# Hybrid pooling and retention step on one core: keys and values turned by VectorE in 32 by 32 blocks instead of by TensorE

## The reference

```python
proj = jnp.einsum('bld,de->ble', rmsnorm(x, g_norm), w_in)      # 1024 -> 10240 columns
u_p, z_p, q, k, v, z_r, gates = jnp.split(proj, IN_SPLITS, axis=-1)
qh, kh = rope(q), rope(k) * RET_QK_DIM ** -0.5                  # 4 heads of 256
o, s_new = retention(qh, kh, vh, s0)                            # values: 4 heads of 512
# one chunk: scores = q @ k.T * decay;  o = scores @ v + (q * decay) @ s
#            s_new  = decay * s + k_dec.T @ v
y_ret = (groupnorm(o) * gn_ret * silu(z_r)) @ w_branch_ret
x_out = x + (sigmoid(gate_p) * y_pool + sigmoid(gate_r) * y_ret) @ w_out
```

## Time and profile before

| | |
|---|---|
| median of three runs | 2835.89 us (2834.78 to 2838.54) |
| profiled execution | 2833.37 us, its span 2831.6 us |
| projection / rest of the span | up to about 1690 us / from there |
| TensorE busy | 2782.2 us, 98% |
| VectorE, ScalarE, GpSimd busy | 64%, 40%, 24% |
| DMA, mean over the span | 195 GB/s |

### The profile page before, as it was taken

One profiled execution on the slowest core, in us unless ns is written; L12 is line 12 of the kernel. 1 busy time (PEld: TensorE's weight loads), 2 busy tenths in 40 slices (PEclk: granted clock), 3 DMA queues, 4 the chain that ended last, 5 costly groups with the idle time before them and its releaser, 6 DMA issues.

```text
span 2831.6 us, 36714 instructions
## 1 busy us (share of the span) xinstructions
PE 2782.2 (98%) x13504; PEld 2249.1 (79%) x13504; DVE 1808.3 (64%) x2588; ACT 1126.4 (40%) x1901; POOL 684.8 (24%) x456
## 2 busy tenths in 40 slices
PE   6999999999999999999999999999999999999998
PEld 5888888888877777777777787877887888788876
DVE  8667566667555365655755566676677667766775
ACT  5444444444554444443434433333333333333332
POOL 5253433434332223425334330000000000000000
PEclk9999999999999999999999999999999999999999
DMA  4544444454564344453444458487648764876496
GB/s 144 197 146 155 173 147 158 156 179 145 180 223 153 113 156 162 147 186 125 163 154 154 165 200 307 141 278 289 246 145 283 289 239 150 283 290 234 153 340 261
DMA packets 281849, 552.80 MB, mean 195 GB/s; under 512 B 24216, under 2 KB 166872, under 8 KB 270527
## 3 DMA queue, kind: packets, MB, share of 16 engines
q1 hardware_dynamic: 266279, 541.73, 53.5%
q10 hardware_dynamic: 15168, 8.46, 1.0%
q0 software_dynamic: 224, 0.26, 0.0%
HBM read 375.59 MB, written 175.14 MB: 194 GB/s over the span
## 4 chain that ended last, share of the span: by engine, by line
PE 90%; DVE 4%; DMA 2%; issue 2%; ACT 1%; POOL 0%; ACTq 0%; SPq 0%; DVEq 0%; POOLq 0%
PE bank L1310 28%; PE bank L1312 28%; PE bank L1311 28%; PE bank L1360 2%; PE bank L1383 1%; PE bank L1502 1%; DMA raw<-in_w_branch_ret 1%; DVE w_lo L2173 1%; DVE xa_lo L2173 1%; DVE xs L2187 1%; PE bank L1632 1%; PE bank L1620 0%; PE bank L1610 0%; DMA x_d<-x_out 0%; DMA raw<-in_w_branch_pool 0%
## 5 line engine op out<-in xcount | busy, mean ns | idle before, releaser
L1310 PE MATMUL bank<-xa_hi,wa_hi 128*128 128x512 f32 x2240 | 888.8, 397 | 5.5 <-ACT part_s L1864 3.2
L1312 PE MATMUL bank<-xa_hi,wa_lo 128*128 128x512 f32 x2240 | 873.6, 390 | 0.0
L1311 PE MATMUL bank<-xa_lo,wa_hi 128*128 128x512 f32 x2240 | 873.5, 390 | 0.0
L1310 PEld LDWEIGHTS bank<-xa_hi,wa_hi 128*128 128x128 f32 x2240 | 420.6, 188 | 107.8 <-issue 21.5
L1312 PEld LDWEIGHTS bank<-xa_hi,wa_lo 128*128 128x128 f32 x2240 | 420.5, 188 | 90.0
L1311 PEld LDWEIGHTS bank<-xa_lo,wa_hi 128*128 128x128 f32 x2240 | 421.1, 188 | 82.8
L2173 DVE TENSOR_TENSOR wa_lo<-w_raw,wa_hi 128x512 fp32r<-128x512 f32 x320 | 312.7, 978 | 165.9 <-ACT wa_hi L1857 165.1
L2173 DVE TENSOR_TENSOR wa_lo<-w_sum,wa_hi 128x512 fp32r<-128x512 f32 x240 | 194.2, 809 | 241.3 <-ACT wa_hi L1857 241.3
L2173 DVE TENSOR_TENSOR w_lo<-raw,w_hi 128x512 fp32r<-128x512 f32 (+1 forms) x288 | 181.9, 659 | 189.3 <-ACT w_hi L1971 189.2
L1857 ACT ACTIVATE wa_hi<-w_raw 128x512 fp32r<-128x512 f32 x320 | 201.2, 629 | 242.6 <-PE bank L1312 238.3
L1971 ACT ACTIVATE w_hi<-raw 128x512 fp32r<-128x512 f32 (+1 forms) x288 | 166.4, 603 | 306.6 <-PE bank L1312 208.5
(11 more groups left out here) (253 smaller groups left out, 4311.8 us busy)
## 6 DMA issues: line engine op xcount, KB each, us to landing
w_raw<-in_w_in SPq DMA_DIRECT2D x80, 1024.0 KB, 5.3
v_d<-turned SPq DMA_DIRECT2D x64, 512.0 KB, 3.2
qk_s<-qk_d SPq DMA_DIRECT2D x32, 1024.0 KB, 7.4
v_s<-v_d SPq DMA_DIRECT2D x32, 1024.0 KB, 11.5
raw<-in_w_branch_ret SPq DMA_DIRECT2D x128, 256.0 KB, 4.2
tabs<-in_c_rope SPq DMA_DIRECT2D x16, 1024.0 KB, 6.9
qk_d<-high SPq DMA_DIRECT2D x32, 512.0 KB, 4.6
qk_d<-c_low SPq DMA_DIRECT2D x32, 512.0 KB, 5.4
```

The source lines that it names most:

```text
L1310: pe.matmul(out, lh, rh, start=first, stop=False, skip_group_check=onto)
L1311: pe.matmul(out, lh, rl, start=False, stop=False, skip_group_check=onto)
L1312: return pe.matmul(out, ll, rh, start=False, stop=last, skip_group_check=onto)
```

## The change

Keys and values are no longer turned by TensorE. VectorE transposes 32 by 32 blocks: a [128, 512] tile becomes 4 by 16 blocks, each turned in its own place. A turned tile then has, in the 32 partitions of quadrant a, tokens of a block and, along the row, the features of quadrant a of all blocks; so what one token needs lies in four quadrants. The DMAs put that together: each group is stored by four DMAs of 32 partitions (keys by eight, high and low apart), in runs of 256 bytes for keys and 512 bytes for values, where one DMA of 128 partitions stood before. Rotated queries and keys have their rows in another order, so their stores are cut into four as well. The columns of the v jobs' weights are taken in blocks of 32, so that the two halves of a job hold alternate blocks. Values are turned in place in `c_out`, keys into `tabs`. `turn_high` and `turn_low` read these tiles instead of PSUM.

The work behind a job is spread over two jobs by `turn_steps`: (steps of the transposes), (steps of the groups), where steps from 7 on lie in the second job behind it.

```diff
-        turned = at("turned", [P, TURNED, 2, 2, DK], F32R)
+        turned = at("turned", [P, TURNED, 8, 2, 2, BT], F32R)
...
             else:
                 engine.wait_ge(rope_done, 2 * before(i, "q", "k") + 2)
+                if kind(i) == "k":
+                    engine.wait_ge(turn_lo, 4 * before(i + 1, "k", "v"))
...
-            if before(j - 1, "k", "v"):
-                engine.wait_ge(turn_mm, 4 * before(j - 1, "k", "v"))
+            if j >= 2 and kind(j - 2) == "k":
+                engine.wait_ge(blocks_turned, 4 * before(j - 1, "k", "v"))
+            if j >= 2 and kind(j - 2) == "v":
+                engine.wait_ge(turn_lo, 4 * before(j - 1, "k", "v"))
+
+        def turn_steps(j):
+
+            blocks_at, groups_at = {("v", 0): ((0, 1), (1, 2, 3, 4)), ("v", 1): ((1, 2), (3, 4, 5, 6)),
+                                    ("k", 0): ((2, 3), (5, 6, 7, 8))}[kind(j), JOBS[j][2]]
+            return blocks_at, groups_at
...
+            def group_store(j, q):
+
+                what, i, part = JOBS[j]
+                n = 4 * before(j, "k", "v") + q
+                b, c = 2 * (j // NJ) + q // 2, q % 2
+                sp.wait_ge(turn_lo, n + 1)
+                for a in range(BA):
+                    src = turned[a * BT:(a + 1) * BT, n % TURNED].bitcast(F32)
+                    if what == "v":
+                        dst = v_d[b, i, 2 * c:2 * c + 2, :, part, a].rearrange("n (b r) x -> r (n b) x", b=BA)
+                        sp.dma_start(dst, src.rearrange("r b h e s -> r b (h e s)"))\
+                            .then_inc(t_stored[n % TURNED], 16)
+                        continue
+                    for low in range(2):
+                        dst = kt_d[b, i, 2 * c:2 * c + 2, :, low, a].rearrange("n (b r) x -> r (n b) x", b=BA)
+                        sp.dma_start(dst, src[:, :, low].rearrange("r b e s -> r b (e s)"))\
+                            .then_inc(t_stored[n % TURNED], 16)
...
+                for low, src in enumerate((qk_high[t], c_low[:, j % 2, t])):
+                    for a in range(BA):
+                        rows = dst[a % 2 * 2 * BT:(a % 2 + 1) * 2 * BT, low, a // 2]
+                        sp.dma_start(rows.rearrange("(e s) t -> s e t", e=2),
+                                     src[a * BT:(a + 1) * BT].bitcast(F32)).then_inc(c_stored[j % 2], 16)
...
                     if what in ("q", "k"):
-                        sp.wait_ge(qk_lo_done, 2 * before(j, "q", "k") + t + 1)
-                        dst = qk_d[b, i, "qk".index(what)]
-                        sp.dma_start(dst[:, 0], qk_high[t][:].bitcast(F32)).then_inc(c_stored[j % 2], 16)
-                        sp.dma_start(dst[:, 1], c_low[:, j % 2, t].bitcast(F32)).then_inc(c_stored[j % 2], 16)
+                        rotated_store(j, t)
+                        if what == "k":
+                            group_store(j, t)
...
+                if j >= 2 and kind(j - 2) == "k":
+                    group_store(j - 2, 2)
+                    group_store(j - 2, 3)
                 if j:
                     store(j - 1)
...
-                    if j and kind(j - 1) in ("k", "v") and 1 <= i < 5:
-                        turn(j - 1, i - 1)
...
+            def turn_blocks(j, t):
...
+                for e in range(2):
+                    src = c_out[:, j % 2, t, e, :]
+                    if kind(j) == "k":
+                        src = src.rearrange("p (c b s) -> p c b s", c=2, s=BT)
+                    dve.transpose(blocks(j, t, e), src).then_inc(blocks_turned, 1)
...
-                        if j and (kind(j - 1), i) in (("q", 2 + 2 * t), ("k", 3 + 2 * t)):
+                        if j and (kind(j - 1), i) in (("q", 2 + 2 * t), ("k", 3 + t)):
                             rope_low(j - 1, t)
```

More of the change, by code:

```diff
@@ L47 @@
 TURNED = 3
+BT = 32
+BA = P // BT
 X_SUM = {S1T1: 0, S2T2: 1, S3T3: 2, S4B22: 3}
@@ L658, in c_free, with turning, weight_columns, like_weights @@
                 stored(engine, j - 2)
-            if before(j - 1, "k", "v"):
-                engine.wait_ge(turn_mm, 4 * before(j - 1, "k", "v"))
+            if j >= 2 and kind(j - 2) == "k":
[6 more added lines that the diff above has]
+            return blocks_at, groups_at
+        def turning(j, i, part):
+            for back in (2, 1):
+                if j >= back and kind(j - back) in ("k", "v"):
+                    at = turn_steps(j - back)[part]
+                    if i + PROD * (back - 1) in at:
+                        yield j - back, at.index(i + PROD * (back - 1))
+        def weight_columns(j, rows, e):
+            w = w_raw[:, j % 2, rows, :]
+            if kind(j) == "v":
+                return w.rearrange("p k (a e s) -> p k a e s", a=BA, e=2)[:, :, :, e, :]
+            return w[:, :, e * P:(e + 1) * P]
+        def like_weights(j, w):
+            return w.rearrange("p k (a s) -> p k a s", a=BA) if kind(j) == "v" else w
+        def blocks(j, t, e):
+            if kind(j) == "v":
+                return c_out[:, j % 2, t, e, :]
+            return tabs[:, :, t * T:(t + 1) * T].rearrange("p c (b e s) -> p e c b s", b=8, e=2)[:, e]
+        def turned_part(j, n, low):
+            return turned[:, n % TURNED, :, low]
+        def turned_source(j, q):
+            t, c = q // 2, q % 2
+            if kind(j) == "v":
+                return c_out[:, j % 2, t, :, c * CHUNK:(c + 1) * CHUNK].rearrange("p e (b s) -> p b e s", s=BT)
+            return tabs[:, c, t * T:(t + 1) * T].rearrange("p (b e s) -> p b e s", b=8, e=2)
         def turn_scale(j):
             return float(gamma[JOBS[j][1]] ** CHUNK) if kind(j) == "k" else 1.0
+        def turned_stores(n):
+            jobs = [i for i in range(ALL) if kind(i) in ("k", "v")]
+            return sum(16 * BA * (2 if kind(jobs[m // 4]) == "k" else 1) for m in range(n % TURNED, n, TURNED))
         def turned_free(engine, n):
@@ L675, in all_turned_stored @@
             for i in range(TURNED):
-                engine.wait_ge(t_stored[i], 16 * len(range(i, n, TURNED)))
+                engine.wait_ge(t_stored[i], turned_stores(n + (i - n) % TURNED))
         def win_steps(sb, g, t):
@@ L1928, in _ @@
                     evict(j, i)
-                    if j and kind(j - 1) in ("k", "v") and 2 <= i < 6:
-                        turn_high(j - 1, i - 2)
+                    for n, q in turning(j, i, 1):
+                        turn_high(n, q)
                     weight_high(PROD * j + i + SLOTS)
@@ L2229, in weight_low @@
                 if i in (S1T1, S2T2, A22T4):
-                    src = w_sum[:, {S1T1: 0, S2T2: 1, A22T4: 1}[i]]
+                    src = like_weights(j, w_sum[:, {S1T1: 0, S2T2: 1, A22T4: 1}[i]])
                 else:
-                    src = {A11B11: w_raw[:, j % 2, 0:KH, 0:P], A12B21: w_raw[:, j % 2, KH:KT, 0:P],
-                           S3T3: w_raw[:, j % 2, 0:KH, P:2 * P], S4B22: w_raw[:, j % 2, KH:KT, P:2 * P]}[i]
-                tt(wa_lo[:, n % SLOTS], src, wa_hi[:, n % SLOTS].bitcast(F32), ALU.subtract, wa_lo_done)
+                    rows = slice(0, KH) if i in (A11B11, S3T3) else slice(KH, KT)
+                    src = weight_columns(j, rows, int(i in (S3T3, S4B22)))
+                tt(like_weights(j, wa_lo[:, n % SLOTS]), src, like_weights(j, wa_hi[:, n % SLOTS]).bitcast(F32),
+                   ALU.subtract, wa_lo_done)
             def tile(j, t, e):
@@ L2357, in _ @@
                     evict(j, i)
-                    if j and kind(j - 1) in ("k", "v") and 2 <= i < 6:
-                        turn_low(j - 1, i - 2)
+                    for n, q in turning(j, i, 1):
+                        turn_low(n, q)
                     weight_low(PROD * j + i + SLOTS)
@@ L2362, in _ @@
                         rope(j - 1, 1, (i,))
+                    for n, t in turning(j, i, 0):
+                        turn_blocks(n, t)
                     if j and kind(j - 1) == "u":
```

126 lines of the change are left out of this document (60 added, 66 removed).

## The result

The changed kernel takes 2849.91 us (median of 4 runs, 2847.93 to 2856.11) against 2835.62 us before: a ratio of 1.0052, 95% interval 1.0034 to 1.007. It is slower by 0.5%, where I had forecast 2802 us and faster. The profiled execution has a span of 2846.1 us against 2831.6.

What follows compares the result with a forecast made beforehand. TensorE, busy 2782.2 of 2831.6 us, was taken as the bound. 2833.4 - 46.5 (transposes) + 3.2 (c22) + 9.6 (stores) = 2799.7 us; the median stood 2.5 us higher, so 2802 us, range 2789 to 2838.

Steps and rivals of the forecast that it cites:

- Transposes gone, -46.5 us: TensorE's projection jobs: without the transposes of keys and values, 5.80 us a head go, 46.5 us over eight heads.
- A transpose at 0.65 us: VectorE: each new [128, 512] transpose takes 0.65 us from start to start, bounds 0.60 to 1.36 us.
- c22 behind k, 3.2 us: Job behind k: VectorE's transposes delay c22, so TensorE's A22T4 waits 0.4 us a head, 3.2 us in all.
- The stores, 9.6 us: SyncE's queue: late stores delay part_s of job u, costing 2.4 us a head in four first-half heads, 9.6 us.
- my own slope: SyncE's queue: each 0.1 us of store spacing s adds 4.5 us a head; x = 45 (s - 0.475).
- The straight line: DMA engines: a line through two measured packet rates gives 20 ns per 256-byte packet, 0.32 us a key DMA, under the issue.
- The 45 issues: SyncE's queue, per head: 45 issues at 0.50 instead of 0.475 us add 1.1 us to the wait for part_s.
- Just in time: Job zp: c22 runs from 35.0 to 35.7 us after k's last product, A22T4 is due at 35.8, so no wait.
- the ride's 2.5 us: Second-half jobs: the sample's ride makes the two jobs between 2.5 us longer, so the stores' 2.4 us a head vanish.
- The small packets: Rival: the keys' 256-byte packets set SyncE's pace; at 40 ns each 2836 us, at 60 ns 2917 us; chance 0.15.
- Half-rate stores: Rival: stores from 32 partitions get half of 404 GB/s, 0.65 us per 128 KB; 2821 us; chance 0.18.
- Values read in runs of 64 columns: TensorE's 672 matmuls of the second part: reading values this way costs 0 to 7 us, taken as 0.

Runs made afterwards that it cites:

- the fastest version: Changed kernel with key parts and channel halves interleaved, half the key stores, whole-tile rotated stores, c22 ahead of the rotated keys' low parts: 2794.92 us, ratio 0.9856.

## Why the prediction was wrong

- **Transposes gone, -46.5 us: right.** Behind the first values a job takes 19.04 and 20.31 us, and in the fastest version all jobs together take the 46.5 us less.
- **A transpose at 0.65 us: right.** It lasts 685 to 688 ns in the mean, and two of them move the next instruction by 1.22 us (276.48 to 277.70). The estimate of 711 ns from the Trainium skill's figure (VectorE: DVE Perf Modes, The three transpose paths) lies 23 to 26 ns above these rows.

```profile
276.48 1.30 DVE L2401 STREAM_TRANSPOSE tabs<-c_out 128x512 f32<-128x512 f32 x2
277.70 1.32 DVE L2235 TENSOR_TENSOR c_low<-c_out,high 128x1024 fp32r<-128x1024 f32 x1
278.95 0.68 DVE L2235 TENSOR_TENSOR c_out<-bank,part_s 128x512 f32<-128x512 f32 x1
```

- **c22 behind k, 3.2 us: right in kind, 8.0 us in size.** c22 starts at 278.95 (the last row above), behind `c_low` as forecast. TensorE stands idle for 0.71 us there (until 279.77), and the job is 1.0 us longer, so a short wait costs some 0.3 us beyond the idle time.

```profile
279.77 0.47 PE L1401 MATMUL bank<-xa_hi,wa_hi 128*128 128x512 f32 x1 [0.71 <-DVE c_out L2235]
```

- **The stores, 9.6 us: this is the step that failed; they cost 48.8 us.** The path was right: `part_s` of the job u stands behind the values' last group, which waits for the store of their first. The size was not. The failed sentence is "I take 0.50 us". In a short run the issue is 0.48 us, but a run of 16 or 24 stores goes out at 0.51 to 0.58 us, and 16 keys with the weights ahead of them at 0.54 to 0.66. From the first rotated store (279.06) to the end of the first group of values (306.18 + 8.71 / 4 = 308.4) it took 29.3 us instead of the 25.1 of my timeline; over the eight heads 28.0 to 29.6, 28.9 in the mean. By my own slope, with x = 3.8, that is 4 x 5.5 + 4 x 3.0 = 34 us lost in all, short of the 46.5 at which the change turns. Measured were 56.8.
- **The straight line did not fail.** With nothing but 256-byte packets of keys going out, between 303 and 306 us, the DMA engines are busy for 61% (the last column but one) and move 109 GB/s. That is some 1280 packets in 3 us, in 29.3 us of busy engines: 23 ns each, against the line's 20. So the packets did not set the pace there; what makes the issue slower in a long run stays open.

```profile
303.00:306.00 3.00, 3.00 (x14) 2.47 (x14) 1.29 (x3) 1.15 (x2) 0.00 (x0) 1.00 0.61 109
```

- **The 45 issues were miscounted.** From the first rotated store to the first group of values there are 32 stores, the weights, 16 keys and 4 values: 53, and 25.1 / 0.475 is 53 too. So 0.1 us of spacing adds 5.3 us a head, and the gain is gone at 0.475 + 5.4 / 53 = 0.577 us, not at 0.595. The forecast itself moves by little more than 1 us.
- **What the slope lacked.** "Just in time" for c22 of the job zp was not in time: the rotated keys land late (13.9 us behind the first rotated store instead of 12.8), VectorE's c11 waits 4.95 us for them, and TensorE waits for c22 in six of the eight jobs zp, 0.3 to 2.1 us each and 5.9 in all. The half clock was no term of the sum at all: during the jobs it lasts 23.9 us in six stretches, which costs half of that, some 12 us. Counted on TensorE, there are 8.0 us behind k, 27.7 of waits for `part_s` of u, 5.9 for c22 of zp, 12 of half clock, and about 4 for what the last 14 waits cost beyond their idle time, at 0.3 each. That makes 57.6 us and so accounts for the 56.8. The second half, where I had let the ride's 2.5 us absorb the delay, lost 3.8 to 5.8 us a head.

```profile
292.98 0.69 DVE L2235 TENSOR_TENSOR c_out<-bank,part_s 128x512 f32<-128x512 f32 x1 [4.95 <-DMA qk_d<-c_low]
...
298.97 0.69 DVE L2235 TENSOR_TENSOR c_out<-bank,part_s 128x512 f32<-128x512 f32 x1
...
299.80 0.47 PE L1401 MATMUL bank<-xa_hi,wa_hi 128*128 128x512 f32 x1 [0.72 <-DVE c_out L2235]
```

All waits of TensorE in the changed kernel for `part_s` and for VectorE's sums. In the first line three waits, 4.4 us in all, stand elsewhere than ahead of u; in the second, eight stand behind k and one elsewhere:

```profile
PE bank L1401 <- ACT part_s L1927: 32.1, 11, 4.9
PE bank L1401 <- DVE c_out L2235: 11.8, 15, 2.1
```

- **Rivals.** The small packets pointed to this loss (0.64 us a store, 2836 us), but packets of twice the size win back only 7.5 us. Half-rate stores are out: values of 128 KB go out every 0.54 us and not 0.65, and the windows from 310 to 316 us moved 233 to 245 GB/s with stores from 32 partitions in flight, so the Trainium skill's 189 GB/s (SBUF — State Buffer, Door 1: The DMA port swizzle) is no limit here, where neighbouring stores leave from different partitions. It is still far below the 404 GB/s of the earlier trace rows, with the DMA engines 94 to 100% busy.
- **Values read in runs of 64 columns, 0 of 0 to 7 us: right as far as the matmuls show.** Those that read them last 389 ns in the median before and after. The matmuls of the state update are busy for 1.9 us more (152.6 against 150.7 us) because eight of them ran at half clock, for up to 628 ns. The part behind the jobs is 3.8 us longer all the same, and the sum had no term for it: TensorE waits 3.3 us instead of 0.7 for the sample's `s_qk`, and 1.3 us for a load of values. What brought these waits stays open, and the profiles of the experiments spread by 5 us in that part.

```profile
PE bank L1597 <- DVE s_qk L2546: 0.7, 1, 0.7
...
PE bank L1660 <- DVE s_qk L2628: 3.3, 1, 3.3
```

## What to carry to other kernels

Price a chain of small stores by the longest stretch of its queue, with whatever bulk load is queued ahead, and not by the spacing of a short run; when the number of stores quadruples, that queue is the resource to count. Look for what stands behind each wait for a free buffer on an in-order engine: moving one eviction ahead of two such waits recovered 40 of the 57 us with no store changed. Here a layout that lets one store carry what two did was worth more than larger packets.

## What was unexpected of the hardware

Six of the eight waits of TensorE ahead of u, 2.5 to 4.9 us long, were followed by a granted clock of 0.5 for 3.4 us, once for 6.8, which added 0.4 to 0.7 of the wait again; two, of 3.2 and 3.3 us, were not. Weight loads of 128 columns took 190 ns from adjacent elements, 194 ns from every second and 312 ns from every fourth; most of that was hidden behind the matmuls (159 us for these three lines instead of 153).
